# Spectrum product of a Hyena layer: real and imaginary rows from one matmul, halves exchanged on ScalarE

## The reference

```python
z = v
for o, g in enumerate((x1, x2)):
    z = g * _bidir_long_conv(z, k_freq[:, o], bias[o])
# _bidir_long_conv:
u_freq = jnp.fft.rfft(u, n=2 * L, axis=1)
y = jnp.fft.irfft(u_freq * k_freq[None], n=2 * L, axis=1)[:, :L]
```

## Time and profile before

| | us |
|---|---|
| median of 3 runs (1436.25 to 1444.73) | 1440.85 |
| profiled execution: its span, the only time it left | 1437.2 |
| TensorE busy in it | 1176.9 (82%) |
| VectorE busy | 844.3 (59%) |
| ScalarE busy | 449.2 (31%) |
| GpSimd busy | 361.9 (25%) |
| mean granted TensorE clock, as a share of full speed | 0.920 |

### The profile page before, as it was taken

One profiled execution on the slowest core, in us unless ns is written; L12 is line 12 of the kernel. 1 busy time (PEld: TensorE's weight loads), 2 busy tenths in 40 slices (PEclk: granted clock), 3 DMA queues, 4 the chain that ended last, 5 costly groups with the idle time before them and its releaser, 6 DMA issues. The chain is left out here.

```text
span 1437.2 us, 14704 instructions
## 1 busy us (share of the span) xinstructions
PE 1176.9 (82%) x5324; PEld 899.6 (63%) x5324; DVE 844.3 (59%) x860; ACT 449.2 (31%) x577; POOL 361.9 (25%) x188
## 2 busy tenths in 40 slices
PE   3698557997686998893885999969999945799995
PEld 1266435886464776672653777748888824588874
DVE  5878468566352575463462576641245436699996
ACT  3356534434332332332342333321111125311110
POOL 0000033100000432330331344431022003244445
PEclk9789858999798999996998999989999988999998
DMA  8779799786677544545787545530101068732221
GB/s 307 244 254 335 273 265 371 259 266 228 191 241 258 192 142 140 171 132 176 228 268 279 176 153 193 182 110 15 43 31 44 30 250 309 259 106 88 88 88 73
DMA packets 143728, 267.92 MB, mean 186 GB/s; under 512 B 23751, under 2 KB 45383, under 8 KB 141386
## 3 DMA queue, kind: packets, MB, share of 16 engines
q1 hardware_dynamic: 142333, 266.45, 54.8%
q10 hardware_dynamic: 1328, 0.59, 0.2%
HBM read 174.72 MB, written 104.60 MB: 194 GB/s over the span
## 5 line engine op out<-in xcount | busy, mean ns | idle before, releaser
L154 PE MATMUL prj_pp<-prj_uhi,prj_whi 128*128 128x512 f32 x768 | 310.9, 405 | 18.3 <-DVE p_pwhl L1618 11.1
L156 PE MATMUL prj_pp<-prj_uhi,prj_wlo 128*128 128x512 f32 x768 | 304.7, 397 | 0.0
L155 PE MATMUL prj_pp<-prj_ulo,prj_whi 128*128 128x512 f32 x768 | 304.4, 396 | 0.0
L154 PEld LDWEIGHTS prj_pp<-prj_uhi,prj_whi 128*128 128x128 f32 x768 | 147.7, 192 | 68.1 <-issue 26.8
L156 PEld LDWEIGHTS prj_pp<-prj_uhi,prj_wlo 128*128 128x128 f32 x768 | 147.2, 192 | 32.2
L155 PEld LDWEIGHTS prj_pp<-prj_ulo,prj_whi 128*128 128x128 f32 x768 | 147.7, 192 | 30.4
L1210 POOL TENSOR_TENSOR p_y<-p_y,p_by_im 128x512 f32<-128x512 f32 x32 | 66.9, 2092 | 262.9 <-DVE p_by_im L1316 184.6
L1307 DVE TENSOR_TENSOR p_ylo<-p_y,p_yhi 128x1024 fp32r<-128x1024 f32 x32 | 56.8, 1773 | 88.0 <-ACT p_yhi L1269 88.0
L154 PE MATMUL out_ps<-whl,out_yhi 128*128 128x512 f32 x256 | 102.2, 399 | 4.7 <-DVE out_ylo L1916 4.6
L628 POOL CAST prj_whi<-prj_ws 128x1024 fp32r<-128x1024 f32 x24 | 28.5, 1189 | 296.6 <-PE prj_pp L156 159.0
L155 PE MATMUL out_ps<-whl,out_yhi 128*128 128x512 f32 x256 | 101.7, 397 | 0.0
(11 more groups left out here) (178 smaller groups left out, 2243.2 us busy)
## 6 DMA issues: line engine op xcount, KB each, us to landing
kseq<-fs_xo SPq DMA_DIRECT2D x32, 512.0 KB, 5.9
p_a<-kseq SPq DMA_DIRECT2D x32, 512.0 KB, 5.6
kfreq<-p_out SPq DMA_DIRECT2D x32, 512.0 KB, 5.5
xseq<-p_xo SPq DMA_DIRECT2D x32, 512.0 KB, 4.2
p_a<-xseq SPq DMA_DIRECT2D x32, 512.0 KB, 5.2
p_kf<-kfreq SPq DMA_DIRECT2D x32, 512.0 KB, 3.6
bseq<-p_out SPq DMA_DIRECT2D x32, 512.0 KB, 5.2
prj_ws<-in_t_win SPq DMA_DIRECT2D x24, 512.0 KB
```

Source lines behind the costliest of these rows:

```text
L154: nc.tensor.matmul(out, w[0], m[0], start=start, stop=False, skip_group_check=True)
L155: nc.tensor.matmul(out, w[0], m[1], start=False, stop=False, skip_group_check=True)
L156: return nc.tensor.matmul(out, w[1], m[0], start=False, stop=stop, skip_group_check=True)
```

## The change

One forward table now holds, in its 128 columns, real rows (0 to 63) and imaginary rows (64 to 127) for one i, so that `fwd` is 2 x 3 matmuls, and `inv` 2 x 3 over all 128 rows. Real and imaginary parts of one bin then lie on different partitions. ScalarE copies `u_ps` with its halves exchanged into `us` (the half that goes up with its sign turned), VectorE multiplies `u_ps` by `k_re` into `y` and `us` by `k_im` in place, and POOL adds the two. Where VectorE and ScalarE both read `u_ps`, they take its two banks in turn. `k_re` (two buffers) and `k_im` (one) hold the filter's rows twice, once on each half, so each is loaded by two transfers of 64 partitions. The order within a step changes on three engines, and SyncE's.

```diff
@@ shape_tables
     def forward(mats):
-        out = np.zeros((P, 4, P))
+        out = np.zeros((P, 2, P))
         for i in range(2):
-            for o in range(2):
-                out[at_row, 2 * i + o, 64 * i:64 * i + 64] = mats[i][:, 64 * o:64 * o + 64]
+            out[at_row, i, :] = mats[i]
...
@@ front
-            for name in ("w1f", "kgen", "kfirst", "f0", "f1", "i0", "i1"):
+            for name in ("w1f", "kgen", "kfirst", "fwd", "inv"):
@@ spectrum_product, SyncE
+            def k_rows(n, o):
+                return kfreq[256 * n:256 * n + 256, :].rearrange("(i r o) c -> o r i c", i=2, o=2)[o]
+            def load_k_re(n):
+                if n < NU:
+                    after(sp, straight_done, 2 * n - 2)
+                    for h in range(2):
+                        sp.dma_start(k_re[n % 2][64 * h:64 * h + 64, :, :], k_rows(n, 0)).then_inc(kre_in[n % 2], 16)
+            def load_k_im(n):
+                if n < NU:
+                    after(sp, turn_done, n)
+                    for h in range(2):
+                        sp.dma_start(k_im[64 * h:64 * h + 64, :, :], k_rows(n, 1)).then_inc(kim_in, 16)
...
             for step in range(S):
                 if step < NU:
+                    load_k_re(step + 2)
+                    load_k_im(step + 1)
+                if 0 <= step - 1 < NU:
+                    store(step - 1)
+                if step < NU:
                     load_a(step + 2)
-                if 0 <= step - 2 < NU:
-                    store(step - 2)
-                if step < NU:
-                    load_k(step + 2)
@@ GpSimd
+            def add(n):
+                pool.wait_ge(straight_done, 2 * n + 2)
+                pool.wait_ge(turn_done, n + 1)
+                nc.gpsimd.tensor_tensor(y[:, :, :], y[:, :, :], us[:, :, :], ALU.add).then_inc(y_done, 1)
             for n in range(S):
                 if n < NU:
-                    nc.gpsimd.tensor_tensor(y[:, 0, :], y[:, 0, :], by_im[:, 1, :], ALU.subtract).then_inc(y_done, 1)
-                    nc.gpsimd.tensor_tensor(y[:, 1, :], y[:, 1, :], by_im[:, 0, :], ALU.add).then_inc(y_done, 1)
+                    add(n)
@@ TensorE
             def fwd(n):
                 pe.wait_ge(alo_done, n + 1)
-                after(pe, mul_done, 2 * n)
+                after(pe, swap_done, 2 * n)
+                after(pe, straight_done, 2 * n)
...
+                for i in range(2):
+                    k = 0 if n == 0 and i == 0 else 1
+                    mm = mm3(nc, u_ps[:, i, :], (fwd_tab[:, k, 0, :], fwd_tab[:, k, 1, :]),
+                             (ahi[:, i, :], alo[:, i, :]), True, True)
@@ ScalarE
+            def swap(n):
+                act.wait_ge(u_done, n + 1)
+                after(act, y_done, n)
+                for i in (1, 0):
+                    if i == 0:
+                        act.wait_ge(straight_done, 2 * n + 1)
+                    nc.scalar.activation(us[0:64, i, :], u_ps[64:128, i, :], ACT.Copy, scale=-1.0)
+                    nc.scalar.activation(us[64:128, i, :], u_ps[0:64, i, :], ACT.Copy).then_inc(swap_done, 1)
...
+            ahigh(0)
             for step in range(S):
                 if step < NU:
-                    ahigh(step)
-                if 0 <= step - 2 < NU:
-                    evac(step - 2)
-                if 0 <= step - 1 < NU:
-                    yhigh(step - 1)
-                (reads of turned tiles, if due)
+                    swap(step)
+                    ahigh(step + 1)
                 (to_row or silu of chunk step - 1)
+                if 0 <= step - 1 < NU:
+                    evac(step - 1)
+                (reads of turned tiles, if due)
+                if step < NU:
+                    yhigh(step)
@@ VectorE
+            def straight(n):
+                dve.wait_ge(u_done, n + 1)
+                dve.wait_ge(kre_in[n % 2], 32 * (n // 2) + 32)
+                after(dve, ylo_done, n)
...
+                for i in range(2):
+                    if i == 1:
+                        dve.wait_ge(swap_done, 2 * n + 1)
+                    nc.vector.tensor_tensor(y[:, i, :], u_ps[:, i, :], k_re[n % 2][:, i, :], ALU.mult).then_inc(straight_done, 1)
+            def turned(n):
+                dve.wait_ge(swap_done, 2 * n + 2)
+                dve.wait_ge(kim_in, 32 * n + 32)
+                nc.vector.tensor_tensor(us[:, :, :], us[:, :, :], k_im[:, :, :], ALU.mult).then_inc(turn_done, 1)
+            alow(0)
             for step in range(S):
                 if step < NU:
-                    alow(step)
+                    straight(step)
+                    turned(step)
+                    alow(step + 1)
                 (conv or gate, if due)
-                if 0 <= step - 1 < NU:
-                    ylow(step - 1)
                 if step < NU:
-                    multiply(step)
+                    ylow(step)
```

More of the change, by code:

```diff
@@ L108, in backward @@
         for i in range(2):
-            for o in range(2):
-                out[64 * o:64 * o + 64, i, at_row] = mats[o][64 * i:64 * i + 64, :]
+            out[:, i, at_row] = mats[i]
         return out
@@ L323, in _ @@
             sp.wait_ge(rows_out, 16)
-            sp.wait_ge(copied, 7 * 16)
+            sp.wait_ge(copied, 5 * 16)
         @block.gpsimd
@@ L1132, in spectrum_product @@
         alo = s.sb("alo", [P, 2, DH], F32R)
-        kf = [s.sb(f"kf{b}", [P, 2, DH]) for b in range(2)]
+        k_re = [s.sb(f"k_re{b}", [P, 2, DH]) for b in range(2)]
+        k_im = s.sb("k_im", [P, 2, DH])
         y = s.sb("y", [P, 2, DH])
-        by_im = s.sb("by_im", [P, 2, DH])
+        us = s.sb("us", [P, 2, DH])
         yhi = s.sb("yhi", [P, 2, DH], F32R)
@@ L1232, in inv @@
                 if n == 0:
-                    pe.wait_ge(i_in, 32)
-                tab = inv_tab[1 if n else 0]
+                    pe.wait_ge(i_in, 16)
                 for i in range(2):
-                    for part, (w, m) in enumerate(((0, yhi), (0, ylo), (1, yhi))):
-                        for o in range(2):
-                            rows = slice(64 * o, 64 * o + 64)
-                            mm = nc.tensor.matmul(b_ps[:, o, :], tab[rows, i, w, :], m[rows, i, :],
-                                                  start=i == 0 and part == 0, stop=i == 1 and part == 2,
-                                                  skip_group_check=True)
+                    k = 0 if n == 0 and i == 0 else 1
+                    mm = mm3(nc, b_ps[:, i, :], (inv_tab[:, k, 0, :], inv_tab[:, k, 1, :]),
+                             (yhi[:, i, :], ylo[:, i, :]), True, True)
                 mm.then_inc(b_done, 1)
@@ L1295, in _ @@
                         gt.silu(act, c // 8, c % 4)
+                if 0 <= step - 1 < NU:
+                    evac(step - 1)
+                if tn and step - 1 in turn_at:
+                    i = turn_at[step - 1]
+                    for part in range(4):
+                        if 4 * i + 6 + part // 2 == step - 1:
+                            tn.read(act, i, part)
+                if step < NU:
+                    yhigh(step)
         @block.vector
```

83 lines of the change are left out of this document (30 added, 53 removed).

## The result

The changed kernel takes 1461.47 us (median of four runs, 1458.54 to 1466.75) beside 1441.04 for the kernel before (1436.25 to 1444.73): ratio 1.0136, 95% interval 1.0105 to 1.0166. It is slower, by 20 us where 12 were forecast (1453). That is inside the stated range (1436 to 1474) and 0.5 us above the narrower one that the prediction gave its own case (1446 to 1461). The profiled span is 1459.8 us against 1437.2, so the two profiles hold the difference.

The account below looks back on a forecast made before the run. The loop through VectorE, ScalarE and POOL (9.05 us, step taken as 8.9) was to bound p3 and p5 instead of TensorE. With events and edges p3 +9.2 and p5 +2.8, together +12: span 1449.2, forecast 1453 us, range 1436 to 1474.

Parts of the forecast that it names:

- its own case: The prediction's main case, "As computed", for the whole kernel: 1453 us, own range 1446 to 1461, chance 0.53.
- convolution: Convolution steps, no longer hidden by slack: +12.1 us three times in p3 (36.3), +9.1 twice in p5 (18.2).
- 15 plain steps: Steps without irregular events in p3 and p5: 8.9 us each, the middle between 9.05 and 8.7.
- weight split: Split on POOL holding up ylo: +2.2 us in unit 1 of each stage, +0.6 in unit 9 of p5.
- reads behind vx stores: p3, units 8 and 12: reads wait for stores ahead of yhi, +4.1 us each, 8.2 in all.
- The loop: p3 and p5: the chain through VectorE, ScalarE and POOL grows from 8.37 by 0.7 to 9.05 us and bounds the step.
- The other order: p3 and p5: if ahi's load is late, the sum runs before alo, and the step is 8.7 us.
- the prediction's last sign of trouble: p5: a granted clock well below 0.95 would mean that TensorE's new gaps cost too.
- The queue behind the row: p3 convolution steps: row, out and yhi queue on ScalarE until the convolution ends, 2.65 us a time.
- Edges: Stage ends: first forward -1.6 us in each of p3 and p5; p3's end -2 (bounds -4 and 0).
- Before the change a step is set by TensorE.: p3 and p5 before the change: TensorE's step of 10.05 us exceeds the other engines' loop of 8.37.
- TensorE stays the bound: Rival: loop under 8.26 us, both stages shrink 1.8 a step, 1398 us; chance 0.13 together with a 1433 variant.

Follow-up runs that it names:

- second deferred version: Changed kernel with y in two buffers, k_re in one, alo ahead of the turned product, yhi and ylo one unit later, inverse matmuls two: 1450.03 us (ratio 1.0052).
- the last version: The second deferred version with the convolution issued one step earlier and the vx stores at the head of SyncE's step: 1408.44 us (ratio 0.9751).
- first deferred version: Changed kernel with y in two buffers, k_re in one, and yhi, ylo, inverse matmuls, out and store one unit later: 1470.97 us (ratio 1.0192).

## Why the prediction was right, and where it was not

The direction and the mechanism held: a loop through the other engines, 0.7 us longer, became the bound, and the irregular events came on top of it. How near the total came owes something to terms that cancel: the convolution was priced 2.7 and 3.7 us too dear, the plain steps and the reads too cheap. And close to a third of the loss came from p4, which the prediction had at nothing. Term by term, in us from the first sum to the last:

| term | p3 forecast | p3 | p5 forecast | p5 |
|---|---|---|---|---|
| 15 plain steps | 133.5 | 135.8 | 133.5 | 135.8 |
| weight split | 2.2 | 2.2 | 2.8 | 2.4 |
| convolution | 36.3 | 33.6 | 18.2 | 14.5 |
| reads behind vx stores | 8.2 | 13.4 | | |
| late loads | | 0.3 | | 1.6 |
| total | 180.2 | 185.2 | 154.5 | 154.2 |

- *The loop.* 9.05 as computed for alo ahead of the sum. The middle of 8.9 was the error. The other order did come, in five steps of p3 and four of p5, where ahi waited for its load, as here in p5; but it was not worth the 8.7:

```profile
926.43 2.38 POOL L1214 TENSOR_TENSOR p_y<-p_y,p_us 128x1024 f32<-128x1024 f32 x1 [5.81 <-DVE p_us L1345]
926.94 2.96 DVE L1318 TENSOR_TENSOR p_alo<-p_a,p_ahi 128x1024 fp32r<-128x1024 f32 x1 [0.65 <-ACT p_ahi L1268]
...
935.47 2.40 POOL L1214 TENSOR_TENSOR p_y<-p_y,p_us 128x1024 f32<-128x1024 f32 x1 [6.66 <-DVE p_us L1345]
```

  That step is 9.04, and six of the nine are 9.04 to 9.07 (the others 9.19, 10.3, and one with stores). The forward matmuls did end 0.35 late, as forecast, but then both pairs of exchange copies stood behind them in the chain, and only the second had been counted: from the first straight product to the turned one the rows have 2.45 us (931.65 to 934.10) instead of 1.96. Also, the pair of exchange copies takes 1.2 us (0.59 and 0.59 to 0.60, starts 0.61 apart), above the 1.07 that was taken, and alo ended 6.80 after E, the end of the sum before, instead of 6.69. TensorE's own step was put at 8.26 and is 8.25 where nothing else binds (second deferred version), though by parts that were misread: the 0.35 ahead of the inverse is about the distance of two starts (815.27 and 815.59), the gap in it 0.1, and forward and inverse take 1.5 each and not 1.37. The clock of p5 fell from 0.99 to 0.93, the prediction's last sign of trouble; the matmuls of plain steps still start 0.23 apart there, so it cost nothing in these.
- *Convolution.* 11.2 and 7.3 a time against 12.1 and 9.1; in p5 the split stood partly beside it. The queue behind the row was seen rightly and is in the trace, but taking it away gave nothing, since TensorE also waits for the projection bank, a wait that the prediction did not have.
- *Reads.* 7.3 and 6.1 instead of 4.1: the stores were issued at 557.47 for 1.89 us, behind the k halves, and the read was released 6.07 after the first issue, 4.3 in the earlier trace rows.
- *Edges.* p3 -4.7 (13.1 less 17.8), forecast -3.6; p5 -0.2 (3.9 less 4.1), forecast -1.6.
- *p4.* The term that was missing, and the largest part of the error: +6.8 of the 10.6 between +12 and the +22.6 of the two spans. p3's reads and loop (+3.9) and p5 (+1.1) are next; the start (-2.0) and the rest (+0.7) nearly cancel.
- *"Before the change a step is set by TensorE."* Right in p5, where the first forward matmuls of the units start 10.05 us apart in 11 of 15 steps (two are 10.91):

```profile
820.05 0.39 PE L154 MATMUL p_u<-p_ahi,p_fwd 128*128 128x512 f32 x1
...
830.10 0.39 PE L154 MATMUL p_u<-p_ahi,p_fwd 128*128 128x512 f32 x1
```

  Behind that even pace the sums are 8.4 to 12.7 apart: the loop falls back at a convolution and catches up at 8.37. That nothing irregular shows in the 150.06 is the slack at work, but little of it is left: 15 x 8.37 = 125.6 and the run with half the forward matmuls took 145.0, so the events use 19.4 of it. In p3 they use 35.9 (161.5 less 125.6), more than 15 x 1.7, and the forwards are 10.05 apart only at the start, then 11 to 14.3. What the prediction had wrong is therefore the worth of a freed TensorE: 11 us in both stages' sums (5.9 + 5.1), and not 1.35 x 32 = 43. Its rival "TensorE stays the bound", 1398, took 15 us off for the convolutions, far too little: the second deferred version, with plain steps of 8.25, took 1450.

In all, against a kernel before with no bound by TensorE (161.5 and 145.0), the changed one is 23.7 and 9.2 us longer: 15 x 0.68 = 10.2 each in plain steps, and 13.5 more in p3, where a convolution costs more by itself (11.2, and 5.4 with 2.2 of split behind it before) and its wait and that for the stores now fall into separate steps (in p5 the events cost 1 less). That TensorE is the bound no more gave back 5.9 and 5.1.

**What p4 shows.** Its matmuls run at 0.23 us from start to start or at 0.43, after waits for xlo of one length. The kernel before, and the one with half the forward matmuls:

```profile
739.62 0.50 PE L154 MATMUL p_zps<-p_xhi,p_itab 128*128 128x512 f32 x1 [1.58 <-DVE p_xlo L1504]
739.96 0.39 PE L155 MATMUL p_zps<-p_xlo,p_itab 128*128 128x512 f32 x1
740.19 0.39 PE L156 MATMUL p_zps<-p_xhi,p_itab 128*128 128x512 f32 x1
```
```profile
737.49 0.60 PE L154 MATMUL p_zps<-p_xhi,p_itab 128*128 128x512 f32 x1 [1.57 <-DVE p_xlo L1502]
737.89 0.63 PE L155 MATMUL p_zps<-p_xlo,p_itab 128*128 128x512 f32 x1
738.32 0.63 PE L156 MATMUL p_zps<-p_xhi,p_itab 128*128 128x512 f32 x1
```

p4 goes in pairs of such groups, 12.1 us from pair to pair. In the changed kernel four pairs have a slow group in the first profile and six in the second, and are 13.65 to 13.75 us long. Over all profiles: 118.2 and 119.6 us at a clock of 0.92 and 0.91 (the kernel before), 121.3 both at 0.88 (the last version, and the one with row and reads behind yhi), 125.0 to 127.8 at 0.82 to 0.86 in the ten others. That the time goes with the granted clock is shown over these 14 profiles, and one profile shows that fewer forward matmuls in p3 bring it about without anything else of the change. What of p3 decides it is open: TensorE's busy share in p3 does not order the cases (0.69 with row and reads behind yhi, p4 121.3; 0.78 with half the forward matmuls, p4 127.8).

## What to carry to other kernels

An engine can set the pace of nearly every step and still be worth little: in p5 TensorE did, and halving its forward matmuls gained 5 us, because the next path, through VectorE, ScalarE and GpSimd, was only 5 us shorter. So add up the next path over the whole stage, its irregular steps listed one by one, and not only its plain step, by which that edit promised 15 x 1.35 = 20. Before work is moved from the full engine to a loop that closes through others, cut the loop: here the same product with the inverse side deferred and the convolution placed where its input is ready is 2.5% faster than before, where the change by itself was 1.4% slower. How much of the 2.5% needs the change is not shown. Where a queued instruction is moved off a wait, look for who else waits for the same thing, here TensorE for the row's bank.

## What the hardware showed that was not expected

- Where a sum or split of GpSimd with two operands in SBUF met these instructions of VectorE, the one that came second was held up, and the wait is recorded as busy time: the sum 3.23 us behind alo and 2.40 alone, alo 3.41 behind the sum and 1.22 alone, the convolution's first part 6.73 with sum and split, 3.99 with the sum only and 1.91 with neither. The Trainium skill says so ("SBUF — State Buffer", section "Who interferes with whom": an exclusive lock, no sharing), and these rows agree. It was the price of a wrong order: 0.83 us of the changed kernel's sum, and more in the first deferred version.
- A wait can slow TensorE in the groups that follow: behind a gap of 2.37 us in p5 of the changed kernel the matmuls' starts went from 0.23 to 0.43 us apart.

```profile
832.49 0.50 PE L151 MATMUL p_b<-p_yhi,p_inv 128*128 128x512 f32 x1 [2.37 <-DVE p_ylo L1324]
832.82 0.42 PE L152 MATMUL p_b<-p_ylo,p_inv 128*128 128x512 f32 x1
...
833.47 0.63 PE L151 MATMUL p_b<-p_yhi,p_inv 128*128 128x512 f32 x1
833.89 0.63 PE L152 MATMUL p_b<-p_ylo,p_inv 128*128 128x512 f32 x1
```
- A copy of 64 partitions by 512 columns out of PSUM, shifted by 64 partitions, takes ScalarE 0.59 us, as one of 128 partitions does (0.60 for the read of the turned tile): half the partitions save nothing.
